# Second mixer: order of projections, RWKV preparation and triangular solve

## The reference, cut to what matters

```
proj = xn @ w_in                       # 1024 x 3328: 1792 RWKV columns, 1536 differential columns
xs   = p + (token_shift(p) - p) * mu   # RWKV part: r, k, v and three low-rank inputs
decay = exp(-c * sigmoid(w0 + tanh(w_lo) @ w_decay_up)); a = sigmoid(a0 + a_lo @ w_iclr_up)
kk = normalised k * k_k; k = k * (1 + (a - 1) * k_a)
state = state * decay + (state @ -kk) (kk * a) + v k   # for each token; y = state @ r
y = groupnorm(y + bonus) * gate
o = softmax(q1 k1) v - lam * softmax(q2 k2) v          # 4 differential heads, causal, ALiBi
h = h + rms_norm(concat(y, rms_norm(o)) @ w_out)
```

## Time and profile before

| | us |
|---|---|
| median of three runs | 2257.58 |
| the profiled execution, its time | 2260.03 |
| its span in the profile | 2257.9 |
| PE busy in the span | 2047.0 (91%) |
| DVE busy | 1048.0 (46%) |
| ACT busy | 755.0 (33%) |
| POOL busy | 162.5 (7%) |
| mean granted TensorE clock | 0.944 of full speed |

### The profile page before, as it was taken

The page is one execution under the profiler, slowest core; times in us unless marked ns, Lnnn a source line. Parts: engine busy times, 40 slices in busy tenths (PEclk is TensorE's granted clock), DMA queues, the critical chain, the costliest instruction groups (busy, mean ns, idle before and its releaser), DMA issues.

```text
span 2257.9 us, 25421 instructions
## 1 busy us (share of the span) xinstructions
PE 2047.0 (91%) x9952; PEld 1673.4 (74%) x9952; DVE 1048.0 (46%) x1458; ACT 755.0 (33%) x1130; POOL 162.5 (7%) x183
## 2 busy tenths in 40 slices
PE   8998999999999989999999979894469789999898
PEld 6875778887887767788887868682369567888786
DVE  5445343333356554343433355546523446666434
ACT  3245332222244545322222242424123234333322
POOL 3000100000011010100000050000011020000000
PEclk9999999999999998999999989997579899999998
DMA  6200123222222010222322322030020012322221
GB/s 185 81 33 6 56 77 109 93 93 87 99 68 69 11 56 20 77 93 93 95 92 93 104 73 75 1 111 1 19 57 1 19 56 87 99 93 93 81 106 37
DMA packets 140700, 158.09 MB, mean 70 GB/s; under 512 B 15945, under 2 KB 129617, under 8 KB 140625
## 3 DMA queue, kind: packets, MB, share of 16 engines
q1 hardware_dynamic: 139328, 155.01, 21.7%
q0 software_dynamic: 1296, 2.05, 0.3%
HBM read 153.36 MB, written 3.68 MB: 70 GB/s over the span
## 4 chain that ended last, share of the span: by engine, by line
PE 85%; DVE 8%; ACT 3%; issue 2%; POOL 1%; DMA 1%; SPq 0%; DVEq 0%; ACTq 0%; POOLq 0%
PE bank L2433 31%; PE bank L2080 16%; PE bank L2454 16%; PE bank L2105 3%; PE bank L2168 3%; PE bank L2196 2%; PE bank L2184 1%; PE bank L2412 1%; POOL arena L787 1%; PE bank L2274 1%; PE bank L2622 1%; PE bank L2341 1%; DVE XL L1358 1%; PE bank L2651 1%; PE bank L2237 1%
## 5 line engine op out<-in xcount | busy, mean ns | idle before, releaser
L2433 PE MATMUL bank<-XH,w_hi 128*128 128x512 f32 x1008 | 398.6, 395 | 0.8 <-DVE w_lo L1621 0.8
L2433 PE MATMUL bank<-XH,w_lo 128*128 128x512 f32 x1008 | 393.4, 390 | 0.0
L2433 PE MATMUL bank<-XL,w_hi 128*128 128x512 f32 x1008 | 393.3, 390 | 0.0
L2080 PE MATMUL bank<-XH,w_hi 128*128 128x512 f32 x528 | 213.1, 404 | 11.9 <-DVE XL L2030 6.5
L2433 PEld LDWEIGHTS bank<-XH,w_hi 128*128 128x128 f32 x1008 | 189.3, 188 | 42.5 <-DVE w_lo L1621 1.6
L2454 PE MATMUL bank<-XH,w_hi 128*128 128x512 f32 x528 | 207.4, 393 | 12.9 <-DVE XL L1608 12.9
L2433 PEld LDWEIGHTS bank<-XH,w_lo 128*128 128x128 f32 x1008 | 189.2, 188 | 40.0
L2433 PEld LDWEIGHTS bank<-XL,w_hi 128*128 128x128 f32 x1008 | 189.4, 188 | 38.3 <-issue 0.5
L2080 PE MATMUL bank<-XH,w_lo 128*128 128x512 f32 x528 | 208.4, 395 | 0.0
L2080 PE MATMUL bank<-XL,w_hi 128*128 128x512 f32 x528 | 208.2, 394 | 0.0
L2454 PE MATMUL bank<-XL,w_hi 128*128 128x512 f32 x528 | 207.1, 392 | 0.0
(11 more groups left out here) (378 smaller groups left out, 3232.2 us busy)
## 6 DMA issues: line engine op xcount, KB each, us to landing
w_raw<-in_ffn_w_gate SPq DMA_DIRECT2D x22, 1024.0 KB, 5.4
w_raw<-in_ffn_w_up SPq DMA_DIRECT2D x22, 1024.0 KB, 5.4
w_raw<-in_ffn_w_down SPq DMA_DIRECT2D x22, 1024.0 KB, 5.0
w_raw<-in_w_up SPq DMA_DIRECT2D x22, 1024.0 KB, 5.0
w_raw<-in_w_in SPq DMA_DIRECT2D x13, 1024.0 KB, 5.3
w_raw<-in_w_down SPq DMA_DIRECT2D x11, 1024.0 KB, 4.8
w_raw<-in_even_w_in SPq DMA_DIRECT2D x9, 1024.0 KB, 5.3
w_raw<-in_even_w_out SPq DMA_DIRECT2D x4, 1024.0 KB, 5.0
```

Source lines behind the costliest of these rows:

```text
L2080: m = pe.matmul(bank[to][0:M, :], cols(w, k), x[:, x0 + k, :], start=(first_k and k == 0 and j == 0), stop=(last_k and k == kt - 1 and j = ...
L2433: m = pe.matmul(bank[b][:, :], w[:, k, P * c:P * (c + 1)], x[:, k, :], start=(k == 0 and j == 0), stop=(k == KT - 1 and j == 2))
```

## The change

The RWKV units come first in `mix2`, the differential units second. The eight small products (`lora_up`) stand behind the first tile of the first differential unit, and the four norm products (`key_sums`) at the ends of the first four differential units. On DVE and ACT the preparation of tile t is interleaved with the evacuation of the differential tiles and the splits of the weights; the products of r and k with the decays go to POOL. The key products now go by tile t (two blocks of four chunks) and stand at the start of attention. The solve stands in attention on DVE behind the maxima of groups 7 to 22, two steps at a time; the clearing of buffers that POOL did stands there too. The buffers are placed anew. In `rwkv_chunks` the transposes of chunk 0 stand ahead of the off-diagonal product, and the transposed attention output is evacuated there through four banks instead of two.

```diff
-            linear("diff_in", w[:, 1792:3328], 1536)
             linear("rwkv_in", w[:, 0:1792], 1792)
+            linear("diff_in", w[:, 1792:3328], 1536)
...
+        ZEROED = 6
+        ABANK = (7, 5, 7, 6)
+        PRE = (4, 5, 7, 4, 5, 7, 4, 5)
...
@@ SP, inverse_blocks
-                sp.wait_ge(rw_ak, NCH)
+                sp.wait_ge(rw_ak, 4)
...
-                sp.wait_ge(rw_zero, 3)
+                sp.wait_ge(rw_zero, ZEROED)
+                sp.wait_ge(at_o, ATT["diff"]["g0"] + len(ATT["diff"]["list"]))
...
@@ POOL
-                    pool.memset(zeroed, 0.0).then_inc(rw_zero, 1)
+                    for t in range(4):
+                        pool.wait_ge(rw_exp, t + 1)
+                        pool.tensor_tensor(rr[:, t, :], rr[:, t, :], RT[:, 4, :], ALU.mult)
+                        pool.tensor_tensor(kk[:, t, :], kk[:, t, :], RT[:, 2, :], ALU.mult).then_inc(rw_rk, 1)
...
@@ ACT, mix2
+                act.wait_ge(shift_in, 14)
+                act.activation(lora0[0:64, :], lora0[0:64, :], ACT.Tanh)
+                act.activation(lora1, lora1, ACT.Sigmoid).then_inc(rw_lora, 1)
+                split(diff[0] + 1)
                 for t in range(4):
                     act.wait_ge(rw_pre, 2 * t + 1)
...
                 exp_and_log()
                 for t in range(4):
                     act.wait_ge(rw_d, t + 1)
+                    if t >= 1:
+                        act.wait_ge(rw_rk, t)
...
                     act.activation(RT[:, 1, :], RT[:, 1, :], ACT.Exp, scale=-0.5, bias=epsb[:, 2:3]).then_inc(rw_rn, 1)
+                    split(diff[t + 1] + 1)
...
+                key_blocks_of(0)
+                key_blocks_of(1)
+                act.wait_ge(rw_rk, 4)
+                attention("diff", lambda n: key_blocks_of(n + 2) if n < 2 else None)
...
@@ DVE, mix2 (the interleaved order, and what stands between the groups)
+                split(diff[0] + 1)
+                query_key(0)
+                for t in range(4):
+                    decays(t)
+                    query_key(2 * t + 1)
+                    key_norm(t)
+                    split(diff[t + 1] + 1)
+                    keys_of(t)
+                    if t < 3:
+                        query_key(2 * t + 2)
...
+                def clear(n):
+                    if n < 3:
+                        inner(n + 1)
+                    for m, lo, hi in ((14, 0, 5), (20, 5, 7)):
+                        if n in (m, m + 1):
+                            x = zeroed.rearrange("p (a b) -> p a b", b=SEQ)[:, 8 * (n - m) + lo:8 * (n - m) + hi, :]
+                            dve.memset(x, 0.0).then_inc(rw_zero, 1)
...
+                    if n == 7:
+                        dve.wait_ge(inv_in, 16)
+                    if 7 <= n < 23:
+                        solve_step(2 * n - 14)
+                        if n < 22:
+                            solve_step(2 * n - 13)
...
+                inner(0)
+                attention("diff", clear)
+                dve.memset(zeroed.rearrange("p (a b) -> p a b", b=SEQ)[:, 7, :], 0.0).then_inc(rw_zero, 1)
+                dve.wait_ge(sub_rstd, 1)
...
@@ PE, mix2
+                for u in tok_units("diff_in"):
...
+                            if t == 0 and j == 0:
+                                lora_up()
+                            if t == 1:
+                                key_sums(j)
...
+                inner(0)
+                attention("diff", lambda n: inner(n + 2) if n < 2 else None)
...
+            def key_sums(t):
+                pe.wait_ge(rw_sqs, t + 1)
                 pe.wait_ge(rw_sig, 8)
...
@@ PE, rwkv_chunks
                 keys(0)
+                turn(0)
                 off_diagonal(0)
-                turn(0)
                 inverse(0)
+                pe.wait_ge(ot_lo, ot_base["mix2"] + 4)
```

More of the change, by code:

```diff
@@ L1372, in head_pairs_out, with attention @@
                                              ALU.mult, ALU.subtract).then_inc(ot_lo, 1)
-            def attention(name):
+            def attention(name, between=lambda n: None):
                 A = ATT[name]
@@ new lines, in value @@
+                def value(j):
+                    at = 256 * (j // 4)
+                    dve.wait_ge(lin_ready, L + 8 + j + 1)
+                    dve.tensor_scalar(vd[j % 4][:, at:at + 256], bank[(L + 8 + j) % 4][:, 0:256], rcol[:, j % 4:j % 4 + 1],
+                                      None, ALU.mult).then_inc(lin_free, 1)
+                split(diff[0] + 1)
+                query_key(0)
+                for t in range(4):
+                    decays(t)
[5 more added lines that the diff above has]
+                        query_key(2 * t + 2)
@@ new lines, in mix2 @@
+                dve.wait_ge(rw_keys, 4)
+                dve.wait_ge(rw_pre, 8)
+                dve.memset(ABD, 0.0).then_inc(abd_zero, 1)
+                dve.tensor_tensor(facl[:, :, 0:NCH - 1], cend[:, :, 0:NCH - 1], cmid[:, :, 1:NCH], ALU.add)\
+                   .then_inc(rw_facl, 1)
+                for j in range(4):
+                    value(j)
+                split(diff[5] + 1)
+                for j in range(4, 8):
+                    value(j)
+                L += 16
+                strict = C("strict").unsqueeze(1).broadcast_to([P, NCH, CH])
@@ L1998, in rwkv_chunks @@
                 keys(0)
+                for t in range(4):
+                    dve.wait_ge(ot_hi, ot_base["mix2"] + t + 1)
+                    dve.scalar_tensor_tensor(XL[:, 4 + t, :], bank[t][:, :], subg, XH[:, 4 + t, :].bitcast(F32),
+                                             ALU.mult, ALU.subtract).then_inc(ot_lo, 1)
                 inverse(0)
@@ L2201, in attention @@
                 scores(0)
+                between(-1)
                 scores(1)
@@ L2581, in mix2 @@
                         columns("pre")
+                for u in tok_units("diff_in"):
+                    j = u - first["diff_in"]
+                    unit(u)
+                    for t in range((2, 2, 2, 2, 4, 4)[j]):
+                        free(L)
+                        if j < 4:
+                            feature_tile(u, KT, 256, whole(P * t), P, 0, L).then_inc(lin_ready, 1)
+                            if t == 0 and j == 0:
+                                lora_up()
+                            if t == 1:
+                                key_sums(j)
+                        else:
+                            token_tile(u, KT, 256, lambda w, k: w[:, k, :], 256, 0, t, L).then_inc(lin_ready, 1)
+                        L += 1
+                    tick(u)
                 pe.wait_ge(lin_free, L)
                 pe.wait_ge(alibi_loaded, 16 * 16)
[L2584 to L2589 removed]
+                inner(0)
+                attention("diff", lambda n: inner(n + 2) if n < 2 else None)
+                for t in range(4):
+                    pe.wait_ge(ot_ready, t + 1)
+                    for i in range(ST):
+                        m = pe.transpose(bank[t][:, P * i:P * (i + 1)], otok_d[:, i, P * t:P * (t + 1)], ident)
+                    m.then_inc(ot_turned, 1)
                 rwkv_chunks()
@@ new lines, in lora_up @@
+                for n in range(8):
+                    t, part = divmod(n, 2)
+                    if n >= 3:
+                        pe.wait_ge(rw_sig, n - 2)
+                    r = slice(64 * part, 64 * part + 64)
+                    pe.matmul(bank[PRE[n]][:, :], wup[r, 0, P * t:P * (t + 1)], lora0[r, :],
+                              start=True, stop=True).then_inc(rw_pre, 1)
+            def key_sums(t):
+                pe.wait_ge(rw_sqs, t + 1)
+                pe.wait_ge(rw_sig, 8)
+                if t >= 1:
+                    pe.wait_ge(rw_max, t)
+                pe.matmul(bank[7][:, :], C("half_ones"), RT[:, 1, :], start=True, stop=True).then_inc(rw_sum, 1)
@@ L2623, in rwkv_prepare, with inner @@
+            def inner(t):
+                if t == 2:
+                    pe.wait_ge(rw_ak, 1)
+                for b in range(2 * t, 2 * t + 2):
+                    pe.wait_ge(rw_abd, b + 1)
+                    for e in range(4):
+                        c = 4 * (b % 2) + e
+                        m = pe.matmul(bank[ABANK[t]][:, CH * c:CH * (c + 1)], ABD[:, b % 2, e, :],
                                       KRk[:, t, chunk(c)], start=True, stop=True)
```

369 lines of the change are left out of this document (171 added, 198 removed).

## The result

| | before | after |
|---|---|---|
| median | 2258.22 (2256.8 to 2258.98, 4 runs) | 2207.0 (2203.16 to 2212.08, 4 runs) |
| profiled execution | 2260.03 | 2203.16 |
| its span | 2257.9 | 2201.4 |
| PE / DVE / ACT / POOL busy | 2047.0 / 1048.0 / 755.0 / 162.5 | 2046.6 / 1049.7 / 756.0 / 168.1 |
| mean granted clock | 0.944 | 0.957 |

What follows compares the result with a forecast made beforehand. Bound by 124 us of VectorE, ScalarE and DMA latency between projections and chunk loop, TensorE waiting. 1406.7 + 96 + 90 + 20.6 puts the first inverse at 1613.3 against 1660.35, 47 us gained: 2211 us, range 2190 to 2234.

Steps and rivals of the forecast that it cites:

- T: Start of attention, when the last differential unit is done: forecast 1502.7, 96 us after the RWKV units end.
- mark, first inverse: End of the first inverse, after which both kernels do the same work: 1613.3 forecast against 1660.35, a gain of 47 us.
- Part 1, the swap: Projections: putting the RWKV units first costs and gains nothing in itself; the six RWKV units take 67.4 us.
- Part 2, the turn of 17.1: Preparation beside differential units: VectorE and ScalarE waiting in series, not TensorE, set 17.1 us a turn; stall 28.5 us.
- the low-rank step: Early in the differential units: TensorE leaves the eight small products 13.2 us after the RWKV units, a stall of 7.7.
- POOL's products at nothing: Beside the differential units: moving products of r and k to POOL costs nothing, hidden by splits; uncovered 3.1 us a turn.
- Part 3, attention at 90: Attention with key products and solve: VectorE binds from group 7 to 22; 90 us to the end of the clearing.
- Rival B: Attention stays one round trip through four engines, each added instruction lengthening it: 112 us, total 2233; chance 0.14.
- rival A: Everything hides: projections stall only 7.7 us and attention costs 78, total 2178; chance 0.10.
- The blocks' trip: Attention: the blocks' way through DRAM takes 8.4 us of 9 left before group 7; 10 us late gives 2221, chance 0.05.
- Part 4, the tail at 20.6: Between attention's last clearing and the first inverse: scaling, bonus weights, keys, masks, transposes, products and copy in series, 20.6 us.
- rival D: Every stall drops TensorE to half clock and it never gets back: 2295, slower than before; chance 0.03.

Runs made afterwards that it cites:

- e1: Changed kernel with ScalarE's split of the weights ahead of its exps in turns 1 to 3, not behind them; 2196.17 us, ratio 0.9725.
- e4: Changed kernel with 30 of the 31 solve steps left out, so the inverse isn't computed; 2197.3 us in one run.
- e3: Changed kernel with ScalarE copying the transposed weights twice in groups 7 to 22 of differential attention; 2206.4 us in one run.
- e2: Changed kernel with fifteen clearings of 512 columns moved from VectorE to POOL; 2202.32 us, ratio 0.9759.
- e9b: Changed kernel with VectorE closing each half head of differential attention one group later; 2199.63 us, ratio 0.9736.
- e8: Changed kernel with e10, e2, e9b and e7 together, plus the clearing of the solve's target on POOL; 2177.8 us, ratio 0.9648.
- e7: Changed kernel with chunk 0's keys ahead of the output's transposes, its key blocks made earlier, bonus weights and last clearing moved into attention; 2193.93 us, ratio 0.9716.
- e10: e1 with VectorE emptying the next tile's accumulators before making `w_lo` in turns 1 and 2, not after; 2196.49 us.

## Why the prediction was right, step by step

| step | forecast | profile after |
|---|---|---|
| t0, end of the RWKV units | 1406.7 | 1404.2 |
| first turn, next turns | 18.7, 17.1 | 17.9, 16.94 |
| t0 to T | 96 | 93.9 |
| a group in the solve's stretch | about 3.5 (60.1 / 16 in the sum) | 3.66 |
| T to the end of the last clearing | 90 | 89.8 |
| tail | 20.6 | 19.4 |
| mark, first inverse | 1613.3 | 1607.22 |

The mark came 6.1 us sooner than forecast: 2.5 by t0, 2.1 by stage 2, 0.2 by attention and 1.2 by the tail. The first of these is no step of the change: the restart of TensorE fell at 1337.04 instead of 1339.34, out of the part ahead of the mixer that differs between executions. With 3.4 us behind the mark, the profiled span is 9.5 below forecast; the median of four runs is 4 below.

**Part 1, the swap, costs nothing.** Right: the RWKV units took 67.10 us of TensorE in 67.10 at a clock of 0.99, against 67.4.

**Part 2, the turn of 17.1.** Right in size and in cause (its terms add up to 17.2, not 17.1). Two scans and the wait for the split between them, 16.94 us apart with 3.26 us of it, are the series that was added up:

```profile
1435.26 1.22 DVE L2027 TENSOR_TENSOR_SCAN arena<-arena 128x512 f32<-128x512 f32 x1
...
1443.61 2.29 DVE L1377 TENSOR_TENSOR w_lo<-w_raw,w_hi 128x2048 fp32r<-128x2048 f32 x1 [3.26 <-ACT w_hi L910]
...
1452.20 1.22 DVE L2027 TENSOR_TENSOR_SCAN arena<-arena 128x512 f32<-128x512 f32 x1
```

e1 took the split out and got 7.7 us. TensorE's waits before the norm products are there, in the stage's list of waits (sum, times, longest):

```profile
PE bank L2710 <- DVE arena L2022: 9.2, 3, 4.8
```

They were 1.08, 4.80 and 3.26 us long; near 5 was forecast for units 2 and 3, which fits one of them. Mis-sized is the low-rank step: TensorE was to leave the eight products at t0 + 13.2, a stall of 7.7 us; it left them at 1415.49, t0 + 11.3, which is 5.8. The prediction had them start behind ScalarE's split; they started at 1409.70, as soon as their inputs were there, and six of the sixteen instructions ran before the first sigmoid (1411.24). The table loads and activations ahead of them took 1405.67 to 1409.53, 3.86 us, as before (1541.62 to 1545.48; the 3.96 of the prediction runs on to TensorE's start). The Trainium skill, "ScalarE: Activation LUTs", section "What ACT_TABLE_LOAD costs", would have them longer by its drain, by an estimate of 2.8 us from its 1.38 a load; the second trace disagrees with it as the first did.

**POOL's products at nothing.** Right for this kernel, and right for the reason given: the splits cover them. Each took 1.28 to 1.30 us, not 1.53. The mean in the earlier trace rows mixes six products of 1.27 us and one of 3.14, and that one began 0.3 us after VectorE's `w_lo`, in the kernel before:

```profile
1331.59 3.14 POOL arena L787
```
```profile
1331.29 2.31 DVE L1351 TENSOR_TENSOR w_lo<-w_raw,w_hi 128x2048 fp32r<-128x2048 f32 x1 [8.85 <-ACT w_hi L890]
```

So the slowdown that e1 met was in the trace before the change. The cost without cover had been put at 3.1 us a turn, as waiting; in e1 it was 1.9 us a turn, and it came as slower operations on both engines, which the prediction had not thought of.

**Part 3, attention at 90.** The size is right by luck, the reason half so. The prediction had VectorE bind from group 7 to 22, all 23.7 us of the solve paid, with 2 us of waits. Measured there were 43.47 us busy of 52 (84%; over 85% was the sign named), 4.5 of waits for PE and 1.3 us of gaps ahead of memsets. e4 shows 13.2 of 23 us paid, e3 shows 59% of ScalarE's added time paid, e2 about half of VectorE's, and each of these shares contains a change of the clock. The failing step is "I expect VectorE to bind": a large part of what holds the stage up is VectorE's order, in which closing a half head waits for PE's last outputs. e9b moved that one call by a group, the waits fell from 11.4 to 3.0 us and attention by 5.5. The sum came out right by two errors that cancel: without the solve the prediction's attention is 90 - 23.7 = 66.3 us, where e4 has 76.07 and about 0.5 more to the end of the clearing, so the groups themselves were put some 10 too low and the solve 10.5 too high. Rival B (112) is refuted at 89.8, and so is rival A (78).

**The blocks' trip** was over in time: no wait for a DMA at the first step in the changed kernel. e9b and e8 show how little room there was, 2.0 and 2.2 us.

**Part 4, the tail at 20.6.** 19.4, with two errors against each other. From the clearing to the keys 3.5 us were put, scaling and bonus weights on VectorE, and it took 4.7 (1587.83 to 1592.55). Scaling took 3.43 us instead of 2.5, beside POOL's copies and products:

```profile
1587.91 3.43 DVE L1994 TENSOR_TENSOR under_split<-under_split,small 128x512 f32<-128x512 f32 x4
```

In e2 and e7 the same four instructions took 2.50 while POOL stood idle. But that is not the whole of it: TensorE's transposes of the attention output, which the prediction laid beside this path, stand ahead of the keys in its queue (L2682, 1588.75 to 1592.52 in the chain above) and end with the bonus weights (1592.41). In e2, where the bonus weights were done 1.2 us sooner behind the last sum of squares, the keys started only 0.4 sooner. The inverse and off-diagonal products took 1.16 and 0.89 us instead of 1.71 and 1.89; the clock was 1.00 at the inverse. Half of the tail was needless in this order, as e7 shows with 9.6 us; the prediction took the order as given and asked nothing of it.

**The clock (rival D).** 0.95 over stage 2, 0.72 in the solve's stretch and 0.54 in the tail. It fell where TensorE waited: after 4.80 us of idling at 1451 the norm products and the first matmuls behind them ran at half speed, 2.08 us for two where 1.02 is the time at full speed, and from 1454.5 on the projection was fast again. After 1.08 us of idling at 1434 the clock had not fallen: the two norm matmuls took 1.12 us. The case in which it never gets back did not happen.

## What to carry to other kernels

When two stages are laid beside each other, the chain of the one that waits decides the gain: add up one turn of it across the engines, each instruction from its row, before asking which engine is busiest. In a stage where TensorE and VectorE are both around 80% busy, look for the instruction that waits in order ahead of others that could run; moving one call by a group (e9b) took 5.5 us off attention, moving 6.2 us of work to an idle engine (e2) 3.5. After a reorder, ask of each thing on the new tail what it truly needs: the keys of chunk 0 needed nothing of the last half head, and that was worth most of 9.6 us. And before an interval's change is put down to an edit, look at the clock in it: the tail moved by up to 2.6 us with no edit in it.

## What the chip showed that was not expected

- VectorE and GpSimd slow each other when both run products of two SBUF operands: 2.29 to 3.06 us and 0.69 to 1.77 on VectorE, 1.30 to 3.34 on GpSimd (e1). The ends of these rows fit engines that take turns, a whole instruction at a time. Where VectorE began first, in the kernel before, it took 2.31 and GpSimd 3.14. With one operand in PSUM on VectorE's side neither was slower (e10: 0.69 and 1.29). A scaling of four tiles with one large SBUF operand and one small one took 3.43 us beside GpSimd and 2.50 without (e2, e7).
- A memset of 2560 columns on VectorE took 2.19 us, with 0.47 us of idle time ahead of it that nothing releases ("issue"); both such memsets of the changed kernel show it, and its two of 1024 columns (0.91 us) have 0.15 and 0.16:

```profile
1546.83 2.19 DVE L1960 MEMSET arena<- 128x2560 f32 x1 [0.47 <-issue]
...
1552.07 2.19 DVE L1960 MEMSET arena<- 128x2560 f32 x1 [0.48 <-issue]
```

- The intervals inside the mixer repeat to 0.02 us between two executions of one kernel, while the 750 us ahead of that first RECIPROCAL differ by up to 7.6 us and the part behind the mixer's inverse by 5.7. On this kernel an interval is a sharper measure than the time.
- The tail of one and the same instructions took 21.52, 19.92 or 17.34 us, at a mean granted clock of 0.50, 0.57 and 0.70, depending on edits ahead of it.
